# A seven-product first feed-forward block, and all modulation as 1024-column pieces spread over the blocks

## The chip, the core and the metric
The kernel runs on one core of one Trainium2 chip. The metric is the device time of one execution in microseconds. TensorE does the matrix products; VectorE, ScalarE and GpSimd compute beside it; SyncE's queue issues nearly all DMAs, in program order, and waits in place when one of them has to wait. TensorE's granted clock is given as a share of full speed.

## The reference
One inference step of a model of two layers, on 512 latent and 128 context tokens of width 1024. A layer has three residual blocks: a feed-forward block, a mixing block and a second feed-forward block. The mixing block is attention with an mLSTM in layer 0, and a gated short convolution in layer 1. Six blocks follow one another:

```python
def modulation(cond, w, b):
    m = jax.nn.silu(cond) @ w + b
    return m.reshape(cond.shape[0], 1, N_MOD, D_MODEL)
def modulate_in(x, g_pre, mod, j):
    return rmsnorm(x, g_pre) * (1.0 + mod[:, :, 3 * j + 1]) + mod[:, :, 3 * j]
def gated_residual(x, out, g_post, mod, j, weight):
    return x + weight * mod[:, :, 3 * j + 2] * rmsnorm(out, g_post)
def swiglu(h, w13, w2):
    a, g = jnp.split(h @ w13, 2, axis=-1)
    return (jax.nn.silu(g) * a) @ w2
```

The modulation of a layer is nine groups of 1024 columns (shift, scale and gate of each of its three blocks), for two condition vectors, latent and context. Its weight matrix is 1024 by 9216 for each layer. D is 1024 and the hidden width of a feed-forward block is 2816.

## The kernel before, in words
The blocks are numbered s = 0 to 5: feed-forward, mixing ("ab"), feed-forward, feed-forward, short convolution ("sc"), feed-forward. Every matrix product is made with three matmuls: each float32 operand is split into a high part (ScalarE copies it, `w_hi`) and the rest (VectorE subtracts, `w_lo`), and high times high, high times low and low times high are summed.

A feed-forward block has two halves of 11 hidden tiles (`HF`). Each half has an in-phase and an out-phase. In the in-phase a pair of units makes one hidden tile: the two weight tiles of 128 columns for g and a, against 640 tokens in two parts of 320. A unit is 8 times 3 times 2 matmuls of 320 columns, a plain pair 96. A seven-product pair makes the same tile from seven products of half-size blocks (4 times 3 matmuls each, 84 in all). Its operands are sums of blocks: VectorE and GpSimd add weight blocks (`w_sum`), and once for a block VectorE and GpSimd add blocks of the activations (`t_sum`), split into `t_hi` and `t_lo`. The table `PLAIN` says which blocks use it: in those the first half has 3 plain and 8 seven-product pairs, the second half 11 seven-product pairs. Block 0 is not among them: all its 22 pairs are plain.

The out-phase has units of 15 matmuls of 512 columns (five token tiles, three matmuls each). In a second half's out-phase seven of the units for the second 512 columns are held back (`held_hi`, `held_lo`), so that TensorE can finish the output tile after tile, and the next block's normalisation and transposes are placed between these tiles. What this does is the boundary to the next block.

Raw weights have two slots. The load of unit n waits in SyncE's queue for the split of unit n − 2 (`w_lo_ok`), ScalarE's split of unit n waits until TensorE has finished unit n − 2 of an in-phase (n − 4 of an out-phase), and TensorE waits for VectorE's split.

The modulation is made in two ways. In block 0 (`JOBS`) layer 0's last seven groups are made in 28 steps of 256 columns: VectorE multiplies a weight tile with the condition vector's column and accumulates, 16 instructions a step, then transposes and adds (`job_half`, `job_turn`), and TensorE sums over the partitions (`sum_jobs`). For layer 1 (`MODS`) a piece of 1024 columns takes eight steps (`add_step`): each loads a tile of 512 KB (`ada_tile`) and has two VectorE instructions of 1024 columns, one for each condition vector. After a step the semaphore `ada_used` goes up; the load of tile j waits for step j − 3. TensorE then sums the accumulators with 8 matmuls of 256 columns in four column groups (`modulation`), VectorE adds the bias to four rows (`modulation_rows`), SyncE stores them to DRAM (`modulation` there), and the block that needs them loads them as columns (`load_cols`) or as gate rows (`load_gate`). The tables `LOADS`, `STEPS`, `SUMS_AT`, `ROWS_AT`, `STORE_AT` give the unit of an out-phase (in the sc block: of its in-phase) at which each of these stands in its engine's program. The sc block has 24 in-units; units come in threes, and VectorE computes the convolution of a group (`u_pad`, `y_conv`) among the splits.

The first two groups of layer 0 are made in the opening, with `cond_silu` as TensorE's stationary operand, two columns wide.

## Time and profile before

| | |
|---|---|
| three runs, median | 2480.43 us |
| lowest and highest | 2480.0 and 2482.57 us |
| the profiled execution, from its first to its last instruction (its own time; the profile gives no other) | 2483.0 us |
| TensorE busy in it | 2419.5 us |
| VectorE, ScalarE, GpSimd busy | 1773.0, 907.4, 351.1 us |
| mean granted TensorE clock | 0.994 |

Busy time of an engine says little by itself. The windows table cuts the span into stages, and the timeline rows say which engine waited at a place and for whom: a bracket at the end of a row holds the idle time before it and what ended it. A row with xN merges N instructions.

### The profile page before, as it was taken

Reading aid. Unit: us, or ns where it says so; the run is one execution under the profiler, and the core shown is the slowest. Engines: PE = TensorE matmul, PEld = TensorE weight load, DVE = VectorE, ACT = ScalarE, POOL = GpSimd, SP = SyncE. Lnnn points to the kernel's source line nnn. Section 1 sums busy time; section 2 is a strip of 40 time slices with the busy share of each in tenths; the row PEclk is TensorE's granted clock in tenths of the full one; section 3 lists DMA queues with packets and bytes.
Section 4 is the critical chain, followed back from the end, with each engine's and each line's share of the span. In section 5 each row is a group of like instructions: output and inputs, shape, how many; then the busy total and the mean of one; then the engine's idle time right before and its main releaser. Section 6 shows DMA issues by size and latency. Waiting matters only on the chain. (4 is left out here: it accounts for less than half of the span.)

```text
span 2483.0 us, 38913 instructions
## 1 busy us (share of the span) xinstructions
PE 2419.5 (97%) x14856; PEld 2227.7 (90%) x14856; DVE 1773.0 (71%) x2701; ACT 907.4 (37%) x1740; POOL 351.1 (14%) x373
## 2 busy tenths in 40 slices
...
GB/s 246 163 141 136 124 152 165 132 120 145 67 57 73 93 98 94 64 221 98 86 143 96 86 70 211 102 86 107 98 145 137 106 84 100 69 146 101 86 107 114
DMA packets 359638, 289.76 MB, mean 117 GB/s; under 512 B 38918, under 2 KB 317334, under 8 KB 358454
## 3 DMA queue, kind: packets, MB, share of 16 engines
...
HBM read 275.32 MB, written 12.18 MB: 116 GB/s over the span
## 5 line engine op out<-in xcount | busy, mean ns | idle before, releaser
L2064 DVE TENSOR_TENSOR w_lo<-w_raw,w_hi 128x512 fp32r<-128x512 f32 (+2 forms) x287 | 260.8, 912 | 281.0 <-ACT w_hi L1458 278.0
L1458 ACT ACTIVATE w_hi<-w_raw 128x512 fp32r<-128x512 f32 (+2 forms) x287 | 228.6, 799 | 602.5 <-DMA w_raw<-in_ffn_w_dram 231.4
L969 PE MATMUL psum<-w_hi,act_hi 128*128 128x512 f32 x800 | 319.1, 399 | 4.8 <-DVE w_lo L2064 4.8
L971 PE MATMUL psum<-w_hi,act_lo 128*128 128x512 f32 x800 | 317.1, 396 | 0.0
L970 PE MATMUL psum<-w_lo,act_hi 128*128 128x512 f32 x800 | 317.0, 396 | 0.0
L1044 PE MATMUL psum<-hT_hi,w_hi 128*128 128x320 f32 x1216 | 278.0, 310 | 0.6 <-DVE w_lo L2064 0.4
L1044 PE MATMUL psum<-hT_lo,w_hi 128*128 128x320 f32 x1216 | 277.1, 309 | 0.0
L1044 PE MATMUL psum<-hT_hi,w_lo 128*128 128x320 f32 x1216 | 277.0, 309 | 0.0
L1088 PE MATMUL psum<-hT_hi,w_hi 128*128 128x320 f32 x684 | 211.6, 309 | 1.6 <-DVE z_quarters L2348 1.6
L1090 PE MATMUL psum<-hT_hi,w_lo 128*128 128x320 f32 x684 | 211.4, 309 | 0.0
L1089 PE MATMUL psum<-hT_lo,w_hi 128*128 128x320 f32 x684 | 211.3, 309 | 0.0
L1044 PEld LDWEIGHTS psum<-hT_hi,w_hi 128*128 128x128 f32 x1216 | 203.0, 188 | 3.5 <-DVE w_lo L2064 2.6
L1044 PEld LDWEIGHTS psum<-hT_hi,w_lo 128*128 128x128 f32 x1216 | 203.4, 188 | 0.0
L1044 PEld LDWEIGHTS psum<-hT_lo,w_hi 128*128 128x128 f32 x1216 | 203.2, 188 | 0.0
L969 PEld LDWEIGHTS psum<-w_hi,act_hi 128*128 128x128 f32 x800 | 150.6, 188 | 46.5 <-DVE w_lo L2064 8.9
L971 PEld LDWEIGHTS psum<-w_hi,act_lo 128*128 128x128 f32 x800 | 150.6, 188 | 36.7
L970 PEld LDWEIGHTS psum<-w_lo,act_hi 128*128 128x128 f32 x800 | 150.7, 188 | 35.4
L2033 DVE SCALAR_TENSOR_TENSOR mod_acc<-ada_raw,cond_silu,mod_acc 128x256 f32<-128x256 f32 x392 | 159.9, 479 | 0.0
L1088 PE MATMUL psum<-t_hi,w_hi_more 128*128 128x320 f32 x456 | 140.9, 309 | 0.0
L1090 PE MATMUL psum<-t_hi,w_lo_more 128*128 128x320 f32 x456 | 140.9, 309 | 0.0
L1089 PE MATMUL psum<-t_lo,w_hi_more 128*128 128x320 f32 x456 | 140.8, 309 | 0.0
L1088 PEld LDWEIGHTS psum<-hT_hi,w_hi 128*128 128x128 f32 x684 | 128.4, 188 | 2.3 <-DVE w_lo_more L2310 2.3
...
## 6 DMA issues: line engine op xcount, KB each, us to landing
w_raw<-in_ffn_w_dram SPq DMA_DIRECT2D x116, 512.0 KB, 4.4
w_raw<-in_ffn_w_dram SPq DMA_DIRECT2D x148, 256.0 KB, 2.9
w_raw_next<-in_ffn_w_dram SPq DMA_DIRECT2D x60, 512.0 KB, 5.4
ada_raw<-in_ada_w_dram SPq DMA_DIRECT2D x56, 512.0 KB, 3.6
ada_tile_ffn<-in_ada_w_dram SPq DMA_DIRECT2D x40, 512.0 KB, 4.1
w_raw<-in_ab_w_in_dram SPq DMA_DIRECT2D x28, 512.0 KB, 4.1
w_raw<-in_sc_w_in_dram SPq DMA_DIRECT2D x24, 512.0 KB, 4.0
...
```

Of the source, the lines that this page charges most:

```text
L969: mm(out, a_hi, b_hi, start=first, stop=False)
L970: mm(out, a_hi, b_lo, start=False, stop=False)
L971: return mm(out, a_lo, b_hi, start=False, stop=final)
L1044: last = mm(IN[p][0:width, h, 0:HT], a, b[:, k, h * HT:(h + 1) * HT], start=(k == 0 and a is hi and b is hT_hi), stop=(k == KD - 1 and a i ...
L1088: mm(out, hi[:, k, :], o_hi[:, k, :], start=(k == 0 and q < 4), stop=False, **on)
L1089: mm(out, hi[:, k, :], o_lo[:, k, :], start=False, stop=False, **on)
L1090: last = mm(out, lo[:, k, :], o_hi[:, k, :], start=False, stop=(k == KH - 1), **on)
L1458: A(dst, src, ACT.Copy).then_inc(w_hi_ok, 1)
L2033: ins = V.scalar_tensor_tensor(acc[:, cd, :], w, col, acc[:, cd, :], ALU.mult, ALU.add)
L2064: V.tensor_tensor(d_, a, b.bitcast(F32), ALU.subtract).then_inc(w_lo_ok, 1)
```

## The change
- Block 0 becomes a seven-product block like blocks 2, 3 and 5: 3 plain and 8 seven-product pairs, then 11.
- The 256-column steps are gone. The gate of block 0 (group 2 of layer 0) is multiplied on TensorE: eight tiles of 512 KB (`ada_direct`), four in flight, and 32 matmuls of 256 columns with `cond_silu` stationary, 16 behind unit 3 and 16 behind unit 5.
- The other six groups become pieces in the manner of layer 1's, and layer 1's groups move along. Pieces in the first and second half or block: block 0 has 2 and 1, ab 2, block 2 has 2 and 1 (before 2 and 0), block 3 has 2 and 1 (before 2 and 0), sc 3 (before 2), block 5 has 1 and 0. The second half's piece is of kind "rest"; its accumulators and tiles lie in the place of the operand sums and of x.
- In a second half with a piece, three of the five tiles of x are reloaded after the piece's last step, and the next block's columns are loaded after the piece has been stored.
- In the sc block the third piece has its steps at units 18 to 22, its sum in the out-phase after unit 4, its rows at unit 6, its store and the next block's columns ahead of the load of unit 8.

```diff
-PLAIN = {2: (3, 0), 3: (3, 0), 5: (3, 0)}
+PLAIN = {0: (3, 0), 2: (3, 0), 3: (3, 0), 5: (3, 0)}
...
-JOBS = {0: (0, 2 * D, (HF, HF), (3, 3))}
-assert (sum(JOBS[0][2]) + sum(JOBS[0][3])) * JW == NMOD - 2 * D
-MODS = {1: [[(1, 0), (1, D)]], 2: [[(1, 2 * D), (1, 3 * D)], []], 3: [[(1, 4 * D), (1, 5 * D)], []],
-        4: [[(1, 6 * D), (1, 7 * D)]], 5: [[(1, 8 * D)], []]}
-assert sorted(z for q in MODS.values() for y in q for z in y) == [(1, j * D) for j in range(9)]
+GATE0 = (0, 2 * D)
+MODS = {0: [[(0, 3 * D), (0, 4 * D)], [(0, 5 * D)]], 1: [[(0, 6 * D), (0, 7 * D)]], 2: [[(0, 8 * D), (1, 0)], [(1, D)]],
+        3: [[(1, 2 * D), (1, 3 * D)], [(1, 4 * D)]], 4: [[(1, 5 * D), (1, 6 * D), (1, 7 * D)]], 5: [[(1, 8 * D)], []]}
+assert sorted([GATE0] + [z for q in MODS.values() for y in q for z in y]) == [(0, j * D) for j in range(2, 9)] + [(1, j * D) for j in range(9)]
 MW, MODC = 256, 1024
-STEPS = {"ffn": [1 + j for j in range(16)], "ab": [2, 2, 3, 3, 4, 4, 5, 5, 7, 9, 10, 10, 11, 11, 12, 12], "sc": [2 + j for j in range(16)]}
-SUMS_AT = {"ffn": (10, 18), "ab": (6, 12), "sc": (11, 19)}
-ROWS_AT = {"ffn": (13, 21), "ab": (7, 99), "sc": (13, 21)}
-STORE_AT = {"ffn": (15, 99), "ab": (9, 15), "sc": (15, 23)}
-LOADS = {"ffn": [3, 3, 3] + [4 + j for j in range(13)], "ab": [4, 4, 5, 5, 5, 6, 6, 7, 7, 8, 8, 10, 12, 13, 13, 13],
-         "sc": [2, 2, 2] + [4 + j for j in range(13)]}
-LATE = (3, 0)
+STEPS = {"ffn": [1 + j for j in range(16)], "rest": [1 + j for j in range(8)],
+         "ab": [2, 2, 3, 3, 4, 4, 5, 5, 7, 9, 10, 10, 11, 11, 12, 12], "sc": [2 + j for j in range(16)] + [18, 18, 19, 19, 20, 20, 21, 22]}
+SUMS_AT = {"ffn": (10, 18), "rest": (9,), "ab": (6, 12), "sc": (11, 19, 99)}
+ROWS_AT = {"ffn": (13, 21), "rest": (12,), "ab": (7, 99), "sc": (13, 21, 99)}
+STORE_AT = {"ffn": (15, 99), "rest": (13,), "ab": (9, 15), "sc": (15, 23, 99)}
+LOADS = {"ffn": [3, 3, 3] + [4 + j for j in range(13)], "rest": [3, 3, 3] + [4 + j for j in range(5)],
+         "ab": [4, 4, 5, 5, 5, 6, 6, 7, 7, 8, 8, 10, 12, 13, 13, 13], "sc": [2, 2, 2] + [4 + j for j in range(13)] + [17, 17, 18, 18, 19, 19, 20, 21]}
+SC_LAST = (4, 6, 8)
+DIRECT_LOADS = {2: (0, 1), 3: (2, 3), 4: (4, 5), 5: (6, 7)}
+DIRECT_AT = {3: (0, 1, 2, 3), 5: (4, 5, 6, 7)}
...
+            def load_direct(k):
+                if k >= 4:
+                    sp.wait_ge(direct_used, k - 3)
+                else:
+                    sp.wait_ge(xT_ok, NT)
+                layer, col = GATE0
+                src = ada_w[layer].rearrange("(p k) n -> p k n", k=KD)[:, k, col:col + MODC]
+                dma(direct[k % 4][:], src).then_inc(direct_loaded[k % 4], 16)
...
+                        if n < 2:
+                            continue
                         sp.wait_ge(w_lo_ok, n - 1)
                         dma(raw[:, n % 2], src[:, :, col + i * P:col + (i + 1) * P]).then_inc(w_loaded[n % 2], 16)
-                    if i == 0 and done is not None:
-                        store_rows(done)
-                    for t in range(NT) if i == 1 else ():
+                        for k in DIRECT_LOADS.get(n, ()):
+                            load_direct(k)
+                    if s == 0 and i == 1:
+                        load_bias_rows(0, "ffn", *GATE0)
+                    for t in range(NT) if i == 1 and s else ():
...
+                    if s == 0 and g == ph["g0"] + 1 and not ph["half"]:
+                        store_mod_rows(0, "ffn", *GATE0)
+                        load_slow()
...
+                        load_pairs(s, ffn_w13[l, f], ph, c0)
+                        if ph["half"] == 0:
+                            load_out(s, ffn_w2[l, f], c0, ph)
+                            continue
+                        load_out(s, ffn_w2[l, f], c0, ph, 0, 4)
+                        sp.wait_ge(pe_prod, SEVEN * ph["g1"])
+                        sp.wait_ge(mod_stored, STORED(ph["mb"] - 1))
+                        load_gate(s)
+                        if not ph["mods"]:
                             for t in range(NT):
                                 load_out(s, ffn_w2[l, f], c0, ph, 4 + 2 * t, 6 + 2 * t)
-                                dma(X[:, t, :], xd[:, t, :]).then_inc(s_x, 16)
+                                reload_x(s, t)
                             load_out(s, ffn_w2[l, f], c0, ph, 4 + 2 * NT)
                             continue
-                        load_in(ffn_w13[l, f], nb, 0, HF, [FF + c0, c0], P, ph, done)
-                        done = ph if ph["jobs"] else None
-                        if ph["half"] == 1:
-
-                            sp.wait_ge(mod_stored, 16 * ph["bt"])
-                            load_gate(s)
-                            if s + 1 < len(SUBS):
-                                load_cols(s + 1)
-                        elif s == 0:
-                            load_slow()
-                        load_out(s, ffn_w2[l, f], c0, ph)
+                        for t in range(2):
+                            load_out(s, ffn_w2[l, f], c0, ph, 4 + 2 * t, 6 + 2 * t)
+                            reload_x(s, t)
+                        load_out(s, ffn_w2[l, f], c0, ph, 8)
+                        sp.wait_ge(ada_used, USED(AG(ph, 8 * len(ph["mods"]) - 1)))
+                        for t in range(2, NT):
+                            reload_x(s, t)
+                        sp.wait_ge(mod_stored, STORED(ph["mods_end"] - 1))
+                        load_cols(s + 1)
...
+                        sp.wait_ge(mod_stored, STORED(ph["mods_end"] - 2))
+                        sp.wait_ge(ada_used, USED(AG(ph, 8 * len(ph["mods"]) - 1)))
+                        load_gate(s)
+                        load_out(s, sc_w_out[0], 0, ph, 0, SC_LAST[2])
+                        store_mod_rows(ph["mods_end"] - 1, "sc", *ph["mods"][-1])
                         sp.wait_ge(mod_stored, STORED(ph["mods_end"] - 1))
-                        load_gate(s)
                         load_cols(s + 1)
-                        load_out(s, sc_w_out[0], 0, ph)
+                        load_out(s, sc_w_out[0], 0, ph, SC_LAST[2])
...
+            def direct_gate(n):
+
+                for k in DIRECT_AT.get(n, ()):
+                    pe.wait_ge(direct_loaded[k % 4], 16 * (k // 4 + 1))
+                    for i in range(4):
+                        last = mm(PS[32 * i:32 * i + 2, DIRECT_BANK, 0:MW], csil[:, :, k], direct[k % 4][:, i * MW:(i + 1) * MW], start=(k == 0), stop=(k == KD - 1))
+                    last.then_inc(mod_mm if k == KD - 1 else direct_used, 1)
...
+                    elif ph["kind"] == "sc" and u == SC_LAST[0]:
+                        modulation(ph, None, last_of=len(ph["mods"]) - 1)
...
+                                direct_gate(ph["nin"] + 2 * i + r)
...
-            def job_half(ph, q, h, i=0, turn=True):
-
-                j = ph["jb"] + q
-                dve.wait_ge(ada_loaded[h], (i + (j + 1)) * 16)
-                if h == 1:
-                    own.wait_back(0)
-                for k in range(KD // 2):
...
+                    elif ph["kind"] == "sc" and u == SC_LAST[1]:
+                        modulation_rows(ph["mods_end"] - 1, "sc", SUM_BANK["sc"][-1])
...
+                if s == 0 and ph["plain"]:
+                    modulation_rows(0, "ffn", DIRECT_BANK)
```

**SyncE, block 0, units 2 to 5 of the first half.** `w_raw` are the units' weights, `ada_direct` the gate's tiles. After the change:

```order
L584 DMA ada_direct0_146<-in_ada_w_dram 128x1024 [waits xT_ok]
L584 DMA ada_direct1_147<-in_ada_w_dram 128x1024 [waits xT_ok]
L584 DMA w_raw_52<-in_ffn_w13_dram 128x8x128 [waits w_lo_ok]
L584 DMA ada_direct2_148<-in_ada_w_dram 128x1024 [waits xT_ok]
L584 DMA ada_direct3_149<-in_ada_w_dram 128x1024 [waits xT_ok]
L584 DMA mod_bias_ffn_170<-in_ada_b_dram 2x256 x4
L584 DMA w_raw_52<-in_ffn_w13_dram 128x8x128 [waits w_lo_ok]
L584 DMA ada_direct0_146<-in_ada_w_dram 128x1024 [waits direct_used]
L584 DMA ada_direct1_147<-in_ada_w_dram 128x1024 [waits direct_used]
L584 DMA w_raw_52<-in_ffn_w13_dram 128x8x128 [waits w_lo_ok]
L584 DMA ada_direct2_148<-in_ada_w_dram 128x1024 [waits direct_used]
L584 DMA ada_direct3_149<-in_ada_w_dram 128x1024 [waits direct_used]
```

The weights of unit 5 (the third `w_raw`) stand behind two of the gate's tiles that wait for `direct_used`. Before, two 256-column tiles with waits of their own stood between these loads.

**SyncE, block 2, second half's out-phase, from unit 2's weights on.** Before:

```order
L589 DMA w_raw_52<-in_ffn_w2_dram 128x512 [waits w_lo_ok] x2
L589 DMA held_raw0_100<-in_ffn_w2_dram 128x512 [waits pe_unit,act_ready]
L589 DMA gate_56<-modulation 128x2x1024 [waits x_new,mod_stored,pe_prod]
L589 DMA g_post_57<-in_norm_g_dram 128x1024
L589 DMA mod_cols_64<-modulation 128x2x8 x2
L589 DMA g_pre_65<-in_norm_g_dram 128x8
L589 DMA w_raw_52<-in_ffn_w2_dram 128x512 [waits w_lo_ok] x2
L589 DMA x_49<-x_kept_rows 128x1024
L589 DMA w_raw_52<-in_ffn_w2_dram 128x512 [waits w_lo_ok]
```

After, from the wait for the last product on:

```order
L584 DMA mod_bias_rest_172<-in_ada_b_dram 2x256 [waits mrow_ok,pe_prod]
L584 DMA mod_bias_rest_172<-in_ada_b_dram 2x256 x3
L584 DMA ada_tile_rest2_139<-in_ada_w_dram 128x1024
L584 DMA ada_tile_rest0_137<-in_ada_w_dram 128x1024
L584 DMA ada_tile_rest1_138<-in_ada_w_dram 128x1024
L584 DMA held_raw0_93<-in_ffn_w2_dram 128x512 [waits pe_unit,act_ready]
L584 DMA gate_56<-modulation 128x2x1024 [waits x_new,mod_stored,pe_prod]
L584 DMA g_post_57<-in_norm_g_dram 128x1024
L584 DMA w_raw_52<-in_ffn_w2_dram 128x512 [waits w_lo_ok]
L584 DMA ada_tile_rest2_139<-in_ada_w_dram 128x1024 [waits ada_used]
L584 DMA w_raw_52<-in_ffn_w2_dram 128x512 [waits w_lo_ok]
L584 DMA ada_tile_rest0_137<-in_ada_w_dram 128x1024 [waits ada_used]
```

The piece's bias rows and three column tiles (`ada_tile_rest`) came ahead of the held weights and the gate, each further tile came behind a unit's weights, and the block's columns (`mod_cols`, `g_pre`) left this place.

**SyncE, sc block, from unit 16's weights on.** Before (`x7` are units 17 to 23):

```order
L589 DMA w_raw_52<-in_sc_w_in_dram 128x8x128 [waits w_lo_ok]
L589 DMA ada_tile_sc0_148<-in_ada_w_dram 128x1024 [waits ada_used0]
L589 DMA w_raw_52<-in_sc_w_in_dram 128x8x128 [waits w_lo_ok] x7
L589 DMA modulation<-mod_rows_sc_165 2x256 [waits mrow_ok]
L589 DMA modulation<-mod_rows_sc_165 2x256 x3
```

After, from unit 17's weights on:

```order
L584 DMA w_raw_52<-in_sc_w_in_dram 128x8x128 [waits w_lo_ok]
L584 DMA ada_tile_sc2_145<-in_ada_w_dram 128x1024 [waits ada_used]
L584 DMA ada_tile_sc0_143<-in_ada_w_dram 128x1024 [waits ada_used]
L584 DMA w_raw_52<-in_sc_w_in_dram 128x8x128 [waits w_lo_ok]
L584 DMA ada_tile_sc1_144<-in_ada_w_dram 128x1024 [waits ada_used]
L584 DMA ada_tile_sc2_145<-in_ada_w_dram 128x1024 [waits ada_used]
L584 DMA w_raw_52<-in_sc_w_in_dram 128x8x128 [waits w_lo_ok]
L584 DMA ada_tile_sc0_143<-in_ada_w_dram 128x1024 [waits ada_used]
L584 DMA ada_tile_sc1_144<-in_ada_w_dram 128x1024 [waits ada_used]
L584 DMA w_raw_52<-in_sc_w_in_dram 128x8x128 [waits w_lo_ok]
L584 DMA ada_tile_sc2_145<-in_ada_w_dram 128x1024 [waits ada_used]
```

Two tiles with waits for `ada_used` now stand between the weights of units 17, 18, 19 and 20, and one behind each of the next.

**VectorE, sc block, from unit 18's split on.** Before:

```order
L2064 TENSOR_TENSOR w_lo_54<-w_raw_52,w_hi_53 128x1024 [waits w_hi_ok,s_dve]
L2503 TENSOR_TENSOR u_tmp_59<-psum,y_conv_88 128x320 [waits pe_unit]
L2503 TENSOR_TENSOR u_tmp_59<-psum,y_conv_88 128x192
L2503 TENSOR_TENSOR u_tmp_59<-psum,y_conv_88 128x128
L2440 CAST act_hi_85<-u_tmp_59 128x640 [waits in_evac1]
L2441 TENSOR_TENSOR act_lo_86<-u_tmp_59,act_hi_85 128x640 [waits s_dve]
L2064 TENSOR_TENSOR w_lo_54<-w_raw_52,w_hi_53 128x1024 [waits w_hi_ok,act_ready]
L2064 TENSOR_TENSOR w_lo_54<-w_raw_52,w_hi_53 128x1024 [waits w_hi_ok]
```

After:

```order
L1947 TENSOR_TENSOR w_lo_54<-w_raw_52,w_hi_53 128x1024 [waits w_hi_ok,s_dve]
L2111 TENSOR_SCALAR mod_acc_sc20_164<-ada_tile_sc2_145,cond_silu_72 128x1024 [waits ada_landed2]
L2111 TENSOR_SCALAR mod_acc_sc21_165<-ada_tile_sc2_145,cond_silu_72 128x1024
L2113 SCALAR_TENSOR_TENSOR mod_acc_sc20_164<-ada_tile_sc0_143,cond_silu_72,mod_acc_sc20_164 128x1024 [waits ada_used,ada_landed0]
L2113 SCALAR_TENSOR_TENSOR mod_acc_sc21_165<-ada_tile_sc0_143,cond_silu_72,mod_acc_sc21_165 128x1024
L2344 TENSOR_TENSOR u_tmp_59<-psum,y_conv_85 128x320 [waits pe_unit]
L2344 TENSOR_TENSOR u_tmp_59<-psum,y_conv_85 128x192
L2344 TENSOR_TENSOR u_tmp_59<-psum,y_conv_85 128x128
L2309 CAST act_hi_82<-u_tmp_59 128x640 [waits in_evac1]
L2310 TENSOR_TENSOR act_lo_83<-u_tmp_59,act_hi_82 128x640 [waits s_dve]
L1947 TENSOR_TENSOR w_lo_54<-w_raw_52,w_hi_53 128x1024 [waits w_hi_ok,act_ready]
L2113 SCALAR_TENSOR_TENSOR mod_acc_sc20_164<-ada_tile_sc1_144,cond_silu_72,mod_acc_sc20_164 128x1024 [waits ada_used,ada_landed1]
```

Two steps of the third piece (`mod_acc_sc20`, `mod_acc_sc21`) came behind unit 18's split and two behind unit 19's; before, the splits of units 19 and 20 stood with nothing between them.

## Rows read from the trace of the kernel before

**Rows 1.** The page, busy time of each engine over the span.
```profile
PE 2419.5 (97%) x14856; PEld 2227.7 (90%) x14856; DVE 1773.0 (71%) x2701; ACT 907.4 (37%) x1740; POOL 351.1 (14%) x373
```

**Rows 2.** Waits of TensorE: waiter, releaser, us in total, times, longest.
```profile
PE psum L969 <- DVE w_lo L2064: 4.8, 8, 1.5
```

**Rows 3.** Windows by stage: window, length, busy time of each engine, clock, DMA.
```profile
56.92:198.43 141.51, 141.06 (x962) 140.80 (x961) 122.46 (x239) 26.82 (x30) 0.00 (x0) 1.00 0.50 143
198.43:276.13 77.70, 77.70 (x337) 62.54 (x336) 43.48 (x87) 14.23 (x22) 0.00 (x0) 1.00 0.42 133
276.13:431.00 154.87, 154.87 (x1057) 154.87 (x1056) 129.45 (x253) 29.54 (x33) 0.00 (x0) 1.00 0.51 153
431.00:534.23 103.23, 100.07 (x496) 82.39 (x495) 75.87 (x123) 42.97 (x97) 18.97 (x33) 1.00 0.34 99
955.29:1054.61 99.32, 98.80 (x674) 98.56 (x673) 85.62 (x120) 47.77 (x86) 23.03 (x14) 1.00 0.25 71
1054.61:1134.68 80.07, 79.90 (x365) 62.54 (x363) 61.04 (x73) 19.14 (x32) 0.00 (x0) 1.00 0.61 196
1134.68:1270.19 135.51, 135.51 (x925) 135.51 (x924) 114.94 (x162) 63.82 (x116) 33.06 (x20) 1.00 0.27 76
1270.19:1370.76 100.57, 98.55 (x492) 82.44 (x491) 51.93 (x65) 43.20 (x96) 18.95 (x31) 1.00 0.42 140
1715.36:1815.60 100.24, 98.55 (x492) 82.42 (x491) 52.10 (x66) 43.10 (x96) 18.71 (x31) 1.00 0.37 119
```

**Rows 4.** Timeline of TensorE, block 2, a piece's sum: start, us, instruction.
```profile
1093.78 1.04 PE L1109 MATMUL psum<-mod_acc_ffn,pick 128*2 128x256 f32 x16
```

**Rows 5.** Timeline of SyncE and VectorE, block 2, first half's out-phase.
```profile
1056.10 1.29 SPq L589 DMA_DIRECT2D ada_tile_ffn<-in_ada_w_dram  x3
1059.89 1.42 DVE L2229 TENSOR_SCALAR mod_acc_ffn<-ada_tile_ffn,cond_silu 128x1024 f32<-128x1024 f32 x2 [1.20 <-DMA ada_tile_ffn<-in_ada_w_dram]
1067.21 0.68 DVE L2064 TENSOR_TENSOR w_lo<-w_raw,w_hi 128x512 fp32r<-128x512 f32 x1
1067.81 2.47 DVE L2231 SCALAR_TENSOR_TENSOR mod_acc_ffn<-ada_tile_ffn,cond_silu,mod_acc_ffn 128x1024 f32<-128x1024 f32 x2
...
1124.17 0.86 DVE L2216 TENSOR_TENSOR mod_rows_ffn<-psum,mod_bias 2x256 f32<-2x256 f32 x2 [3.10 <-PE psum L1109]
```

**Rows 6.** Timeline of VectorE, sc block.
```profile
1929.20 1.22 DVE L2064 TENSOR_TENSOR w_lo<-w_raw,w_hi 128x1024 fp32r<-128x1024 f32 x1
...
1944.86 0.95 DVE L2490 TENSOR_TENSOR u_pad<-psum,silu_g 128x320 f32<-128x320 f32 x3 [4.13 <-PE psum L1044]
...
1948.35 1.23 DVE L2064 TENSOR_TENSOR w_lo<-w_raw,w_hi 128x1024 fp32r<-128x1024 f32 x1
...
1953.08 0.95 DVE L2503 TENSOR_TENSOR u_tmp<-psum,y_conv 128x320 f32<-128x320 f32 x3 [1.82 <-PE psum L1044]
...
1955.45 1.23 DVE L2064 TENSOR_TENSOR w_lo<-w_raw,w_hi 128x1024 fp32r<-128x1024 f32 x1
```

**Rows 7.** Timeline of SyncE and ScalarE, sc block, units 19 and 20.
```profile
1930.46 4.21 SPq L589 DMA_DIRECT2D w_raw<-in_sc_w_in_dram  x2
1930.55 1.06 ACT L1458 ACTIVATE w_hi<-w_raw 128x1024 fp32r<-128x1024 f32 x1 [6.04 <-PE psum L1044]
```

**Rows 8.** The page, DMA issues: count, KB each, median us from issue to landing.
```profile
w_raw<-in_sc_w_in_dram SPq DMA_DIRECT2D x24, 512.0 KB, 4.0
```

**Rows 9.** Timeline, block 2, second half's out-phase: gate's load, TensorE's wait, gate's product.
```profile
1274.73 0.38 SPq L589 DMA_DIRECT2D gate<-modulation  x1
1285.16 0.50 PE L969 MATMUL psum<-w_hi,act_hi 128*128 128x512 f32 x1 [0.77 <-DVE w_lo L2064]
1285.03 2.28 DVE L2082 SCALAR_TENSOR_TENSOR gate<-gate,g_post 128x2048 f32<-128x2048 f32 x1
```

**Rows 10.** Timeline of VectorE, block 2: the same product without and beside GpSimd.
```profile
1271.81 0.83 DVE L2364 TENSOR_TENSOR z_quarters<-z_quarters 128x640 f32<-128x640 f32 x1 [0.59 <-ACT z_quarters L1615]
971.58 1.92 DVE L2364 TENSOR_TENSOR z_quarters<-z_quarters 128x640 f32<-128x640 f32 x1
```

More of the change, by code:

```diff
@@ L37 @@
 PRO = 2 * D // MODW
-JW = 256
 SQ = 32
-JB = JW // SQ
-JOBS_MAX = 14
 EPS = 1e-6
@@ L775, in load_out @@
                         load_mods(ph, u)
-                    z, r = divmod(u - LATE[ph["half"]] if late else u, 3)
-                    if r < 2 and 0 <= z < late:
-                        load_job(ph, jobs + z, parts=(r,))
                     for i in held_at(ph, u):
```

339 lines of the change are left out of this document (82 added, 257 removed).

## The prediction
> **What bounds the kernel now.** I read the busy shares first: TensorE is busy 97% of the span [rows 1]. The waits of TensorE come next: all its waits for split weights in the out-phases make 4.8 us together, in 8 places [rows 2]. So the time is the sum of TensorE's work, plus whatever new waits the change makes. The windows table by stage then gives the price of each stage; its start and end are starts of the first TensorE row of one stage and of the next [rows 3].
>
> The reader is to see three pairs of stages there. Eleven plain pairs (22 units) took 154.87 us, so 14.08 us a pair and 7.04 us a unit; eleven seven-product pairs took 135.51 us, 12.32 a pair. Eight seven-product pairs behind three plain ones took 99.32 us. The first half's out-phase took 77.70 us with the old modulation (22 units, 3.53 us each) and 80.07 us with two 1024-column pieces. The second half's out-phase up to the next block's third unit took 103.23 us in block 0, but 100.57 and 100.24 in blocks 2 and 3.
>
> The sum is made against the profiled span, 2483.0 us. It is 2.6 us above the median of the runs, 2480.43; I subtract the difference from the median.
>
> **The change, block 0, first half.** Before: 10 plain pairs after the first, 141.51 us, and 77.70 us of out-phase, 219.21 together [rows 3]. After:
> - two plain pairs, 28.16 us, and eight seven-product pairs, 99.3;
> - the gate's columns on TensorE: 32 matmuls of 256 columns against a two-column stationary operand. The nearest row is the sum of a 1024-column piece, 8 matmuls of the same form, 1.04 us or 0.98 to the next row's start [rows 4]; four times 0.98 are 3.9 us. They go into four column groups like those, so I take that value; the bounds are 3 and 6;
> - the weights of unit 5. SyncE's queue holds them behind two of the gate's tiles, which wait for the matmuls that follow unit 3. First units end at 56.92, so unit 3 ends at 71.0, and unit 4, behind 2.0 us of gate matmuls, at 80.0. The load of unit 5 goes out at 72.5 behind two 512 KB tiles; a 512 KB load of this form takes 4.0 us alone [rows 8], and three tiles issued together at 1056.10 had the first landed at 1059.89 [rows 5], so I put it at 78.7. ScalarE's split (1.06, [rows 7]) and VectorE's (1.2, [rows 6]) end at 81.0: a wait of 1.0 us (0 to 2.5);
> - VectorE adds the gate's rows (two such additions took 0.86 [rows 5], so four 1.8 us) before the fourth product's weights. Against block 2 it is then up to 1.4 us late, while a seven-product pair leaves it 12.3 minus 10.7 us (85.62 busy in eight pairs) to catch up: 0.5 us. Slow 4-byte loads stand in the queue before the third pair's weights, needed only some 8 us later: 0.3 us (0 to 2.5);
> - the out-phase as in block 2, 80.07.
>
> That is 213.2, a gain of 6.0 us.
>
> **Block 0, second half.** 154.87 becomes 135.51: 19.4 us gained. The out-phase gets one new piece (next part).
>
> **One more piece in the second half's out-phase, blocks 0, 2 and 3.** TensorE: one sum, 1.0 us [rows 4]. VectorE: eight steps in units 1 to 8. A step is 2.4 us (the first 1.4) and a split 0.6 [rows 5], so 3.0 a unit against TensorE's 3.53. The first half already runs so, but here VectorE also has the gate's 2.28 us at unit 4 and the held weights. From the phase's start at 0: the tiles go out at 1.4, behind the bias rows; the first lands 3.8 later as in the first half [rows 5], step 0 ends at 6.6, unit 2's split at 7.2 (needed at 7.05), unit 3's at 10.1, unit 4's weights come as before, behind the 1.5 MB of the gate (TensorE waited 0.77 there, [rows 9]). Then gate 2.28, step 2.4, split 0.6: unit 5's weights are ready 5.3 us after unit 4's, where TensorE needs them after 3.5. Waits: 0.2 + 0.5 + 1.4 + 0.1 = 2.2 us at units 2, 4, 5 and 6, against 0.77 in block 2 and, by its window's 0.33 less [rows 3], 0.44 in block 3. So 1.4 and 1.8 more. Bounds: 0 and 5 each. From unit 6 on VectorE gains half a microsecond a unit.
> The next block's columns are now loaded at the end, behind the rows' store and three tiles of x. TensorE ends the piece's sum at 2.2 + 35.3 + 1.0 = 38.5 and the first output tile at 38.5 + 3.5 + 7.7 = 49.7. From 38.5 on come the rows 1.8, their store and its landing, which I take at 3.5, the columns' issue and landing behind 1.5 MB of x, which I take at 6.7, since gate and columns in this queue made unit 4 wait till 15 from a start at 4.5 [rows 9]: 50.5. VectorE begins the boundary 1 us late; I count half. 0.5 us (0 to 3).
> So block 2 pays 1.0 + 1.4 + 0.5 = 2.9 us and block 3 pays 3.3. Block 0 goes from 103.23 to 100.57 + 2.9 = 103.5, since its own 2.7 us of the old 256-column steps' disturbance go: 0.2 lost.
>
> **The third piece in the short-convolution block.** Its eight steps sit at units 18 to 22, two a unit at first. What is queued behind what decides here. On SyncE the second tile of unit 18 waits for a step that VectorE does after unit 18's split, and unit 19's weights stand behind it; in unit 19 likewise for unit 20's.
> - Unit 17 ends at 1930.5 ([rows 7], what that split waited for) and unit 18's split at 1930.35 [rows 6]. Two steps (1.4 + 2.4) and the convolution's tail (2.37, from 1953.08 to 1955.45) bring VectorE to 1936.4. Unit 19's load goes out at 1932.2 instead of well before 1930.46 [rows 7], lands at 1936.2 to 1937.6, and its two splits end at 1939.1; unit 18 ends at 1937.5. Wait 1.6.
> - Unit 20's load waits for a step behind that split: +2.4 step, +0.5 for the tile's issue, +4.7 landing, +2.2 splits = 9.8, against 7.04 + 1.0 (a sum): wait 1.8.
> - Unit 21 is VectorE's own: product 0.9, two steps 4.8, convolution 2.5 (0.9 and 2.5 together are 1944.86 to 1948.35, [rows 6]), split 1.15 = 9.3 against 7.04: 2.3.
> - Unit 22: rows 1.8, step 2.4, tail 2.3, split 1.15 = 7.6: 0.6.
> Sum 6.3 us (2 if the loads came free, since only the last two waits are VectorE's, unit 21's then 1.2; 10 if each landing takes 1.5 more). In the out-phase: the piece's sum 1.0, and a late weight load, since the queue waits for the rows' store before the columns' load: 1.2 (0 to 3). Block 4 pays 8.5 us.
>
> **Sum.** −6.0 − 19.4 + 0.2 + 2.9 + 3.3 + 8.5 = −10.5 us: 2470 us. The mixing block is left as it is; it has two pieces before and after, at the same units.
>
> **A rule against the change.** VectorE's product of two SBUF tiles took 0.83 us with GpSimd idle and 1.92 us at 971.58, inside eight pairs in which GpSimd was busy 23.03 us [rows 3, 10]. Of the nineteen seven-product pairs of block 0 seventeen will have GpSimd's two weight sums.
> The Trainium skill, "SBUF — State Buffer", section "Who interferes with whom", says that a VectorE instruction with two SBUF inputs and a GpSimd instruction that reads SBUF take an exclusive lock and that the later one blocks fully; the trace agrees with a block of about 1.1 us. If that fell on the path it would be 17 × 1.1 = 19 us and take back the second half's gain.
> Counted from the rows alone: 1.92 − 0.83 = 1.09 us in each of 17 pairs is 18.5 us, and the time would be 2489. But stages with GpSimd's sums ran at 12.32 us a pair with TensorE busy all 135.51 us, so there it is hidden; VectorE's 114.94 us leave room. Chance 0.03.
>
> **The rivals.**
> 1. The sum above, 2464 to 2477. Chance 0.50.
> 2. The new waits are mostly covered. With the lower bounds (block 4 pays 1.9 + 1.0, blocks 2 and 3 pay 1.0 each, block 0's second out-phase gains 1.7, its first half gains 7.8): 7.8 + 19.4 + 1.7 − 2 − 2.9 = 24 us, 2456. For it speaks that TensorE's waits are so small now; against it that unit 21's wait needs only durations of rows. 2456 to 2464: 0.17.
> 3. The waits cost more: block 4 pays 12 (10 + 1 + 1), each second out-phase 2 us more, half a microsecond more at places in block 0: −10.5 + 3.5 + 6 + 1 = 0 net: 2480. For it speaks that loads behind one another in one queue stretched by more than I count; 2477 to 2485: 0.22. No measurable change is mostly this.
> 4. It is slower. Mechanism: in the three second out-phases the first column tiles land late behind the gate's loads and the held weights, VectorE starts its eight steps late, and each microsecond comes back as TensorE's wait at units 2 to 5, since split and step stand in one order. It decides from (2485.4 − 2470) / 3 = 5.1 us a block. A delay of 6 us gives 2488. Against it: the first tile goes out ahead of the gate's load, and in the first half it landed 3.8 us after its issue. 0.08.
>
> **Numbers.** About 0.2%, 5 us, is what measurement can tell. Faster means under 2475.5: rival 2, nearly all of the first case and the least part of the third: 0.69. Same, 2475.5 to 2485.4: 0.20. Slower: 0.11, with the lock. Range: from 2459 to 2480, which leaves out half of case 2, a third of case 3 and case 4, near 0.2.
>
> **What would show it.** In the changed profile: the eight and eleven seven-product pairs of block 0 at 99 to 101 and 135.5 us; the gate's matmuls about 3.9 us; TensorE waiting for split weights about 1 us ahead of unit 5 in block 0, about 1.4 us ahead of unit 5 of the second out-phases, and four waits of 0.5 to 2.5 us in units 19 to 22 of block 4; scaled columns about 1 us after VectorE could have begun a boundary. I would be wrong if seven-product pairs ran above 12.4 us in block 0, if column tiles landed more than 5 us after issue, or if VectorE's double steps were absorbed.

## The result and the profile after

The changed kernel took 2490.61 us (median of six runs, 2489.51 to 2495.45) against 2483.03 for the kernel before (median of six, the three of the forecast among them). The ratio of the means is 1.0037, interval 1.0026 to 1.0049. It is slower. The forecast was 2470 with a range from 2459 to 2480. The profiled executions took 2488.1 and 2483.0 us, 5.1 apart, and the stages below are told in these.

The page's busy times of the changed kernel:

```profile
PE 2406.5 (97%) x14780; PEld 2201.8 (88%) x14780; DVE 1819.7 (73%) x2517; ACT 977.1 (39%) x1901; POOL 413.1 (17%) x409
```

TensorE is busy for 13 us less than before [rows 1], and yet the end comes later: the waits are the subject. The windows table of the changed kernel, with the columns of [rows 3]: block 0 (first half's in-phase behind the first pair, its eight seven-product pairs alone, out-phase; second half's in-phase, out-phase with boundary), the second out-phases of blocks 2 and 3 with boundary, block 4's in-phase and out-phase:

```profile
57.20:191.19 133.99, 131.66 (x930) 128.20 (x929) 115.04 (x147) 57.64 (x97) 28.34 (x16) 1.00 0.34 92
91.31:191.19 99.88, 99.02 (x676) 98.66 (x673) 86.15 (x122) 46.92 (x85) 23.01 (x14) 1.00 0.28 71
191.19:271.11 79.92, 79.89 (x364) 62.54 (x363) 60.95 (x73) 19.02 (x32) 0.00 (x0) 1.00 0.62 196
271.11:406.63 135.52, 135.52 (x926) 135.51 (x924) 114.91 (x162) 63.80 (x116) 33.05 (x20) 1.00 0.27 76
406.63:515.66 109.03, 102.14 (x508) 83.71 (x507) 70.96 (x85) 43.27 (x98) 18.96 (x33) 0.98 0.46 146
1250.44:1358.38 107.94, 102.13 (x509) 83.69 (x508) 72.31 (x85) 43.16 (x96) 18.94 (x31) 0.98 0.50 170
1702.71:1811.61 108.90, 101.90 (x509) 83.62 (x508) 72.64 (x86) 43.16 (x96) 18.72 (x31) 0.98 0.45 149
1811.61:1978.87 167.26, 161.65 (x1091) 158.11 (x1090) 125.47 (x161) 27.04 (x29) 0.00 (x0) 0.98 0.50 151
1978.87:2061.14 82.27, 78.86 (x418) 65.69 (x417) 45.80 (x61) 38.58 (x89) 13.44 (x26) 1.00 0.31 100
```

Block 4 took 158.40 and 82.58 us in the kernel before:

```profile
1815.60:1974.00 158.40, 158.29 (x1091) 155.53 (x1090) 107.46 (x145) 27.06 (x29) 0.00 (x0) 1.00 0.44 133
1974.00:2056.58 82.58, 79.23 (x403) 66.97 (x401) 43.92 (x57) 38.80 (x89) 13.70 (x26) 0.98 0.31 99
```

Against the forecast, term by term (us, minus is gained; before from [rows 3] and the fence above):

| term | forecast | measured |
|---|---|---|
| block 0, first half | −6.0 | 213.91 − 219.21 = −5.3 |
| block 0, second in-phase | −19.4 | 135.52 − 154.87 = −19.4 |
| block 0, second out-phase, boundary | +0.2 | 109.03 − 103.23 = +5.8 |
| block 2, the same | +2.9 | 107.94 − 100.57 = +7.4 |
| block 3, the same | +3.3 | 108.90 − 100.24 = +8.7 |
| block 4 | +8.5 | +8.9 − 0.3 = +8.6 |
| sum | −10.5 | +5.8 |

Three terms of one kind are 15.5 us too small; that is nearly the whole miss. The stages that the table leaves out changed by −0.7 us together.

**Where a boundary loses.** TensorE's waits of the changed kernel; the first row is its waits for the normalised tiles that it transposes:

```profile
PE psum L927 <- DVE part L1990: 16.8, 12, 4.3
PE psum L909 <- DVE w_lo L1947: 9.0, 10, 1.4
PE psum L982 <- DVE w_lo L1947: 7.0, 4, 3.1
```

The timeline of block 2's boundary, SyncE first, then VectorE, then TensorE:

```profile
1285.29 3.53 SPq L584 DMA_DIRECT2D w_raw<-in_ffn_w_dram  x2
1293.17 1.15 SPq L584 DMA_DIRECT2D modulation<-mod_rows_rest  x4
1294.36 0.36 SPq L584 DMA_DIRECT2D w_raw<-in_ffn_w_dram  x1
...
1289.57 0.69 DVE L1947 TENSOR_TENSOR w_lo<-w_raw,w_hi 128x512 fp32r<-128x512 f32 x1
...
1291.38 1.77 DVE L2098 TENSOR_TENSOR mod_rows_rest<-psum,mod_bias_rest 2x256 f32<-2x256 f32 x4
...
1298.23 0.69 DVE L1947 TENSOR_TENSOR w_lo<-w_raw,w_hi 128x512 fp32r<-128x512 f32 x1 [3.76 <-ACT w_hi L1396]
1298.95 3.08 DVE L2020 TENSOR_TENSOR part<-psum,part 128x512 f32<-128x512 f32 x5
1302.52 1.24 DVE L1959 SCALAR_TENSOR_TENSOR mod_cols<-mod_cols,g_pre 128x16 f32<-128x16 f32 x1 [0.49 <-DMA g_pre<-in_norm_g_dram]
...
1314.24 1.80 PE L927 MATMUL psum<-ident,part 128*128 128x128 f32 x8 [3.07 <-DVE part L1990]
1315.69 0.77 PE L909 MATMUL psum<-held_hi,act_hi 128*128 128x512 f32 x1
```

Read it from below. TensorE waits 3.07 us for the first normalised tile. VectorE begins the boundary with five additions at 1298.95, directly behind the split of the last unit's weights, for which it was idle 3.76 us. These weights were issued at 1294.36, behind the store of the piece's rows, and the store waited in SyncE's queue until VectorE had added the rows (1291.38 to 1293.15). The two loads ahead of the store went out by 1288.8, and the last unit's slot was free from 1290.26, when VectorE had split the weights two units before (1289.57 + 0.69): the store held the load for 4.1 us. For the columns, which the forecast took for the late ones, VectorE waited 0.49 us, less than the 1 us that I said.

The first transposes start 15.29 us after the additions (1298.95 to 1314.24). In blocks 0 and 3 it is 15.29 too (456.08 to 471.37, 1752.43 to 1767.72), and in block 0 of the kernel before (475.46 to 490.75): the additions, ScalarE's squares, GpSimd's five gate products, the norm, x, the next norm. This chain took the same time in all four. In the kernel before it ended 0.2 us behind TensorE in block 0. In block 2 it would have ended at 1311.64 + 15.29 = 1326.93, 0.5 us ahead of TensorE, so there was next to nothing left to hide a later start. Of the kernel before, VectorE's additions and TensorE's first transposes in block 0, the same in block 2 with the second transposes, and last the second transposes of block 2 in the changed kernel:

```profile
475.46 3.08 DVE L2137 TENSOR_TENSOR part<-psum,part 128x512 f32<-128x512 f32 x5
490.75 1.16 PE L989 MATMUL psum<-ident,part 128*128 128x128 f32 x8 [0.20 <-DVE part L2107]
...
1311.64 3.08 DVE L2137 TENSOR_TENSOR part<-psum,part 128x512 f32<-128x512 f32 x5
1327.39 1.05 PE L989 MATMUL psum<-ident,part 128*128 128x128 f32 x8
1334.94 1.13 PE L989 MATMUL psum<-ident,part 128*128 128x128 f32 x8 [0.89 <-issue]
...
1322.54 1.13 PE L927 MATMUL psum<-ident,part 128*128 128x128 f32 x8
```

The gap of 0.89 us ahead of the second transposes is gone where TensorE has waited ahead of the first; why is not shown.

The wait isn't all of the price. The first row is the stretch behind it, the second the one behind the longest wait of block 4; the clock is the third number from the end:

```profile
1314.24:1332.00 17.76, 17.76 (x80) 14.64 (x81) 11.02 (x13) 9.22 (x24) 4.41 (x8) 0.90 0.00 0
1936.85:1946.70 9.85, 9.85 (x51) 9.66 (x54) 5.41 (x5) 1.06 (x1) 0.00 (x0) 0.71 0.69 207
```

A mean of 0.90 of 2.4 GHz, with the lower level at 1.2 GHz, is a loss of 0.10 × 17.76 = 1.8 us; behind the wait of 3.10 us in block 4 it is 0.29 × 9.85 = 2.9. The 0.77 us matmul above took 0.40 elsewhere. Block 2's 7.4 us are then: sum 1.0, waits at units 2, 4 and 5 of 0.15 + 0.81 + 1.42 against 0.77 before, 1.6; the boundary's wait 3.1; the clock 1.8; less the gap of 0.9. That is 6.6; the other 0.8 us I can't assign.

### The profile page after: what moved, and what is told of

Read it like the earlier page. It is cut to its first block and busy times, and to the rows that moved or that the text cites. A ratio compares the mean times of both kernels' runs of the same rounds, so it can differ in the third digit from the quotient of the medians.

```text
span 2488.1 us, 38245 instructions
## 1 busy us (share of the span) xinstructions
PE 2406.5 (97%) x14780; PEld 2201.8 (88%) x14780; DVE 1819.7 (73%) x2517; ACT 977.1 (39%) x1901; POOL 413.1 (17%) x409
## 5 line engine op out<-in xcount | busy, mean ns | idle before, releaser
L1396 ACT ACTIVATE w_hi<-w_raw 128x512 fp32r<-128x512 f32 (+1 forms) x249 | 188.1, 760 | 528.7 <-DMA w_raw<-in_ffn_w_dram 247.6
L1947 DVE TENSOR_TENSOR w_lo<-w_raw,w_hi 128x512 fp32r<-128x512 f32 (+1 forms) x249 | 214.3, 862 | 218.8 <-ACT w_hi L1396 217.4
L1028 PE MATMUL psum<-hT_hi,w_hi 128*128 128x320 f32 x912 | 282.2, 309 | 2.4 <-DVE z_quarters L2215 2.4
L1030 PE MATMUL psum<-hT_hi,w_lo 128*128 128x320 f32 x912 | 281.8, 309 | 0.0
L1029 PE MATMUL psum<-hT_lo,w_hi 128*128 128x320 f32 x912 | 281.8, 309 | 0.0
L1028 PE MATMUL psum<-t_hi,w_hi_more 128*128 128x320 f32 x608 | 187.9, 309 | 0.0
L1030 PE MATMUL psum<-t_hi,w_lo_more 128*128 128x320 f32 x608 | 187.9, 309 | 0.0
L1856 POOL TENSOR_TENSOR w_sum<-w_raw 128x512 f32<-128x512 f32 x36 | 54.9, 1524 | 776.8 <-DVE w_lo L2177 776.8
L1028 PEld LDWEIGHTS psum<-hT_hi,w_hi 128*128 128x128 f32 x912 | 171.2, 188 | 3.5 <-DVE w_lo_more L2177 3.3
L982 PE MATMUL psum<-hT_hi,w_hi 128*128 128x320 f32 x608 | 141.3, 314 | 7.1 <-DVE w_lo L1947 7.0
L982 PE MATMUL psum<-hT_lo,w_hi 128*128 128x320 f32 x608 | 139.5, 311 | 0.0
L982 PE MATMUL psum<-hT_hi,w_lo 128*128 128x320 f32 x608 | 139.3, 311 | 0.0
L2231 DVE TENSOR_TENSOR z_quarters<-z_quarters 128x640 f32<-128x640 f32 x76 | 128.4, 1690 | 4.8 <-ACT z_quarters L1554 4.8
```

What stands on the lines that cost most here:

```text
L982: last = mm(IN[p][0:width, h, 0:HT], a, b[:, k, h * HT:(h + 1) * HT], start=(k == 0 and a is hi and b is hT_hi), stop=(k == KD - 1 and a i ...
L1028: mm(out, hi[:, k, :], o_hi[:, k, :], start=(k == 0 and q < 4), stop=False, **on)
L1029: mm(out, hi[:, k, :], o_lo[:, k, :], start=False, stop=False, **on)
L1030: last = mm(out, lo[:, k, :], o_hi[:, k, :], start=False, stop=(k == KH - 1), **on)
L1396: A(dst, src, ACT.Copy).then_inc(w_hi_ok, 1)
L1856: pool.tensor_tensor(S1[:], A21(g), A22(g), ALU.add).then_inc(ws_ok, 1)
```

## The experiments

Each is an edit of the changed kernel, compared with the kernel before in the same runs. "Gained" is against 2490.6. The kernel before had medians of 2483.51 us beside experiments 1 to 4, 2482.02 beside 5 to 8 and 2483.86 beside 9 and 10, so differences between these groups are good to about 1 us.

**1. The store behind the last weights.**

```diff
-STORE_AT = {... "rest": (13,), ...}
+STORE_AT = {... "rest": (14,), ...}
```

> The store of the piece's rows in the second halves of blocks 0, 2 and 3 stands behind the last unit's weights in SyncE's queue, not ahead of them. Theory (queue): the last unit's weights wait for VectorE's rows, their split comes some 4 us late, VectorE begins the boundary behind it, and nothing on the way to the first transposes has slack. Then the three waits of TensorE ahead of the transposes (4.28, 3.07, 3.88 us) fall under 0.5 each and the lowered clock behind them goes too: 12 to 15 us less than the changed kernel, 2476 to 2479, below the kernel before. Rival (late columns): the columns' loads come behind the same store either way, so the three waits stay as they are and the time stays at 2490.

2478.47 us, ratio 0.9981 (0.9972 to 0.9990): 12.1 gained by one number, and faster than the kernel before. Windows of the three second out-phases, and block 2's SyncE and VectorE:

```profile
406.60:511.06 104.46, 100.60 (x508) 82.36 (x507) 70.79 (x85) 43.31 (x98) 18.95 (x33) 1.00 0.46 152
1247.14:1350.76 103.62, 100.30 (x509) 82.40 (x507) 71.09 (x85) 43.13 (x96) 18.95 (x31) 1.00 0.52 177
1694.80:1799.89 105.09, 100.40 (x508) 82.36 (x507) 71.26 (x86) 43.09 (x96) 18.74 (x31) 1.00 0.47 154
```

```profile
1282.60 4.83 SPq L584 DMA_DIRECT2D w_raw<-in_ffn_w_dram  x3
1289.99 1.15 SPq L584 DMA_DIRECT2D modulation<-mod_rows_rest  x4
...
1291.92 3.08 DVE L2020 TENSOR_TENSOR part<-psum,part 128x512 f32<-128x512 f32 x5
1298.26 0.17 DVE L1959 SCALAR_TENSOR_TENSOR mod_cols<-mod_cols,g_pre 128x16 f32<-128x16 f32 x1 [3.27 <-DMA g_pre<-in_norm_g_dram]
```

The three loads now go out together, the clock is 1.00, and the blocks lost 4.6, 4.3 and 3.8 us less. The gap of 0.89 us ahead of the second transposes is back in all three, which is one reason why it is less than wait and clock together. The additions start right behind the last split. The columns are waited for longer than before the edit, 3.27 us against 0.49, and it costs nothing: TensorE waits no more than 0.20 us for the first transposes, since VectorE has nothing else to do while GpSimd's products run. So a late column isn't what the boundary hangs on; the late last weights are.

**2. Columns and x early, store where it was.**

```diff
+early = 11 if s == 0 else 99
-load_out(s, ffn_w2[l, f], c0, ph, 8)
+load_out(s, ffn_w2[l, f], c0, ph, 8, early)
 ... reload_x(s, t) for t in range(2, NT)
+if s == 0:
+    load_cols(1)
+    load_out(s, ffn_w2[l, f], c0, ph, early)
```

> In block 0 alone x's last three tiles and the next block's columns are loaded ahead of unit 11's weights, some 15 us earlier; the rows' store stays ahead of the last unit's weights. Rival (late columns or late x hold VectorE at the boundary): the wait of 4.28 us ahead of the transposes in block 0 goes, blocks 2 and 3 keep theirs, the time is 5 us lower, 2485. Theory (queue): scaled columns come earlier but the wait stays within 0.5 us of 4.28, and the time stays at 2490.

2493.41 us, ratio 1.0042 (1.0028 to 1.0055). VectorE and TensorE at block 0's boundary:

```profile
460.30 3.08 DVE L2025 TENSOR_TENSOR part<-psum,part 128x512 f32<-128x512 f32 x5
463.30 0.16 DVE L1964 SCALAR_TENSOR_TENSOR mod_cols<-mod_cols,g_pre 128x16 f32<-128x16 f32 x1
...
475.60 1.87 PE L932 MATMUL psum<-ident,part 128*128 128x128 f32 x8 [4.48 <-DVE part L1995]
```

The columns are there at once and the wait is 4.48 us, as it was. The rival is out. The early loads stood ahead of unit 11's weights, and TensorE waited 2.0 and 0.9 us there that it had not waited before; these 2.9 us are about what the time lies above 2490.6.

**3. Block 4, the third piece's loads later, its steps where they were.**

```diff
-"sc": [...] + [17, 17, 18, 18, 19, 19, 20, 21]
+"sc": [...] + [17, 18, 19, 20, 20, 21, 21, 22]
```

> Short-convolution block: the third piece's steps stay in their units on VectorE, only its tile loads stand later in SyncE's queue, so that none waits for a step ahead of the next unit's weights. Theory (queue): the wait of 3.10 us ahead of unit 19 goes with the lowered clock behind it (0.71 over 9.85 us), some 5 to 6 us, and the waits of 1.9 and 0.5 us at units 21 and 22, which are VectorE's own, stay: 2485. Rival (VectorE's double steps hold all of these units): the wait at unit 19 stays above 2 us and the time at 2490.

2484.55 us, ratio 1.0004 (0.9995 to 1.0013): 6.1 gained. The in-phase:

```profile
1811.00:1972.28 161.28, 159.11 (x1091) 155.54 (x1089) 125.47 (x161) 27.05 (x29) 0.00 (x0) 1.00 0.52 157
```

Unit 19's wait of 3.10 us is gone with its clock; 1.44 and 0.53 us stay at units 21 and 22. Queue and VectorE each have their own share, and they are apart now: 6.0 and 2.9 us of the 8.9.

**4. Block 4, steps spread.**

```diff
-"sc": [2 + j for j in range(16)] + [18, 18, 19, 19, 20, 20, 21, 22]
+"sc": [2, 3, 4, 4, 5, 6, 7, 7, 8, 9, 10, 10, 11, 12, 13, 13, 14, 15, 16, 16, 17, 18, 19, 20]
```

The load of tile j stands two units behind step j − 3.

> Short-convolution block: all three pieces' steps are spread over units 2 to 20, with two in one unit only where VectorE is idle afterwards (units 4, 7, 10, 13, 16), each tile's load placed so that it never blocks the next weights. Theory: the third piece then costs its sum of 1.0 us and little else, all waits in units 19 to 22 go, 8 us less than the changed kernel, 2482. Rival (24 steps don't fit beside 23 splits and the convolution, whatever their order): the waits move to units 4 to 16 and at least half of the 8.9 us stays, 2486 or more.

2480.50 us, ratio 0.9993 (0.9984 to 1.0002): 10.1 gained. The in-phase:

```profile
1811.12:1968.93 157.81, 157.76 (x1091) 155.53 (x1089) 125.36 (x161) 27.06 (x29) 0.00 (x0) 1.00 0.53 160
```

TensorE is busy in all of it, and VectorE does the same 125.4 us of work. 24 steps fit; their places, and those of their loads, were the cost.

**5. Both edits.** Experiments 1 and 4 together.

> The store behind the last unit's weights and the spread steps of the short-convolution block together. Theory: the two losses are in different blocks and add: 2490.6 minus 12.1 minus 10.1 is 2468.4, ratio 0.994 to the kernel before, TensorE waits over 2 us nowhere behind the mixing block. Rival (one gives back what the other gains, since every block inherits the arrival times of the last): 2473 or more.

2469.31 us, ratio 0.9945 (0.9931 to 0.9958). The sum of the two gains would give 2468.4: they add.

**6. No step beside the gate's product.** On top of experiment 5.

```diff
-STEPS: "rest": [1 + j for j in range(8)]      SUMS_AT: "rest": (9,)
+STEPS: "rest": [1, 2, 3, 5, 6, 7, 8, 9]       SUMS_AT: "rest": (10,)
```

> As e5_store_and_spread, and in the second halves of blocks 0, 2 and 3 no step of the piece in unit 4, in which VectorE also multiplies the gate tile (steps in units 1 to 3 and 5 to 9, the sum a unit later). Theory (VectorE's order): the wait of 1.43 us ahead of unit 5 goes in all three, 4 us less than e5_store_and_spread: 2464.5. Rival (the weights land late, whatever VectorE does, since the DMA engines are 0.9 busy there): the waits at units 4 and 5 stay above 1.5 us together, no gain.

2467.30 us, ratio 0.9936 (0.9922 to 0.9949), 2.0 below experiment 5, within the spread of runs. The wait of 1.43 us at unit 5 went in all three blocks, as the theory had it, and came back at the boundary. VectorE and TensorE, block 0:

```profile
448.83 1.31 DVE L2098 TENSOR_TENSOR mod_rows_rest<-psum,mod_bias_rest 2x256 f32<-2x256 f32 x3 [0.73 <-PE psum L1059]
...
452.57 3.08 DVE L2020 TENSOR_TENSOR part<-psum,part 128x512 f32<-128x512 f32 x5
...
467.85 1.16 PE L927 MATMUL psum<-ident,part 128*128 128x128 f32 x8 [1.36 <-DVE part L1990]
```

From 452.57 to 467.85 it is 15.28 us again. My expectation had not followed the fixed chain. Counted from unit 4's start, VectorE's additions moved by −0.6, +0.4 and −0.1 us against experiment 5, where TensorE saved 1.4. The edit also puts the piece's sum a unit later, and VectorE waits 0.73 us for it ahead of the rows.

**7. The gate's tiles 4 and 5 behind unit 5's weights.** On top of experiment 5.

```diff
-DIRECT_LOADS = {2: (0, 1), 3: (2, 3), 4: (4, 5), 5: (6, 7)}
+DIRECT_LOADS = {2: (0, 1), 3: (2, 3), 5: (4, 5, 6, 7)}
```

> As e5_store_and_spread, and in block 0 the gate's tiles 4 and 5 are loaded behind unit 5's weights, not ahead. Theory: the wait of 0.9 to 1.9 us ahead of unit 5 of block 0 goes and nothing takes its place, 1.5 us less than e5_store_and_spread: 2467. Rival: the gate's matmuls behind unit 5 or the first product's weights then wait for the late tiles, no gain or up to 2 us more.

2467.33 us, ratio 0.9937 (0.9923 to 0.9950), 2.0 below experiment 5, again within the spread of runs. In the trace the wait of 1.90 us that experiment 5 has there is gone: no wait is left ahead of unit 5 of block 0, and none appears at the gate's matmuls.

**8. All four.**

> All four edits of tables together: 2490.6 minus 12.1, 10.1, 4 and 1.5 is 2463, if they add; 2468 if the last two give nothing. Lower than the kernel before by 0.6 to 0.8%.

2464.34 us, ratio 0.9929 (0.9915 to 0.9942). The second out-phases with boundary, and block 4's in-phase:

```profile
404.16:507.51 103.35, 100.14 (x508) 82.50 (x507) 71.07 (x85) 43.31 (x98) 18.95 (x33) 1.00 0.47 154
1242.27:1345.82 103.55, 100.25 (x509) 82.51 (x507) 71.15 (x85) 43.17 (x96) 18.92 (x31) 1.00 0.52 177
1689.67:1793.56 103.89, 100.26 (x508) 82.51 (x507) 71.33 (x86) 43.09 (x96) 18.68 (x31) 1.00 0.47 156
1793.56:1951.36 157.80, 157.75 (x1091) 155.52 (x1089) 125.34 (x161) 27.05 (x29) 0.00 (x0) 1.00 0.54 160
```

**9 and 10. The rows later.** On top of experiment 8. In experiment 9 `ROWS_AT` of the second halves is 13; in 10 the rows stand behind the five additions, with the two further moves that its expectation names.

> As e8_all_four, and VectorE adds the bias to the piece's rows a unit later, in unit 13 of the three second out-phases (in e8_all_four it waited 0.7 us for the sum in unit 12, and the first transposes came 1.4 us late in each boundary). Theory (what VectorE does ahead of its first addition of the boundary is paid by TensorE one for one, once the slack is gone): the waits of 1.4 us ahead of the transposes halve or go, 2 to 4 us less than e8_all_four, 2461. Rival (the boundary's chain starts with the last weights' landing, whatever VectorE does before): no change, 2464.

> As e8_all_four, but the rows stand behind the five additions that begin the boundary, the scaling of the columns behind the first tile's gate product, and x's last tiles ahead of the rows' store. Theory: the additions start 1.8 to 2.5 us earlier and the waits of 1.4 us ahead of the first transposes go, three times: 2460 to 2461. Rival (the columns then land too late for ScalarE's scaled copy of the first transposed tile): new waits of 1 to 4 us ahead of the second transposes or the next block's first unit, 2464 or more.

Experiment 9: 2464.68 us, ratio 0.9924 (0.9910 to 0.9937). The boundary waits went in blocks 0 and 2 and halved in block 3, but unit 4 of block 0's second out-phase waited 2.33 us for weights, against 0.55 in experiment 8; no gain is shown. Experiment 10: 2461.70 us, ratio 0.9910 (0.9895 to 0.9926), the lowest median; its interval overlaps those of experiments 8 and 9. VectorE, block 0:

```profile
450.46 3.07 DVE L2021 TENSOR_TENSOR part<-psum,part 128x512 f32<-128x512 f32 x5
453.46 1.76 DVE L2101 TENSOR_TENSOR mod_rows_rest<-psum,mod_bias_rest 2x256 f32<-2x256 f32 x4
...
460.15 0.37 DVE L1960 SCALAR_TENSOR_TENSOR mod_cols<-mod_cols,g_pre 128x16 f32<-128x16 f32 x1 [2.72 <-DMA g_pre<-in_norm_g_dram]
```

The first transposes waited 0.30 us in block 0 and not in the two others, and the later columns were hidden once more. Unit 4's wait was there too (1.54, 0.56 and 0.60 us); in block 0 it lies between 0.4 and 2.3 in the runs and depends on the landing of its weights, which this study did not pull apart.

## Why the prediction was wrong

- **Block 0's products: right.** Second in-phase 135.52 us against 135.51, out-phase 79.92 against 80.07, the gate's matmuls 3.7 us (71.64 to 73.48 and 89.47 to 91.31) against 3.9, unit 5's wait 1.46 against 1.0. The first half's term is 0.7 off.
- **The step that failed** is "VectorE begins the boundary 1 us late; I count half. 0.5 us (0 to 3)", in three blocks. It followed the rows' store to the columns that stand behind it and left out the weights of the last unit, which stand between them in the same queue, though VectorE's first addition comes behind their split. In its place: the additions start 3.8 us later than with the store behind the weights (456.08 against 452.27 in block 0), TensorE waits 3.1 to 4.3 us, and the lower clock adds 1.7 to 1.8. Moving the store gave back 4.6, 4.3 and 3.8 us, where the forecast had counted 0.5 for the late start. Experiment 1 shows the place, experiment 2 that it isn't the columns. The bound of 3 us had neither the whole delay nor the clock.
- **Rival 4 had the stage and the size right and the mechanism wrong.** It needed 5.1 us a block and gave 2488; the three blocks lost 5.6, 4.5 and 5.4 us above the forecast. But it put the loss at units 2 to 5 by late column tiles. Those waits were 2.4 us in block 2 against 2.2 forecast. I gave it 0.08.
- **The waits at units 2 to 5** were right in size and kind (VectorE's order at unit 5, 1.42 against 1.4). Experiment 6 shows that removing one alone returns most of it at the boundary, which the sum could not have shown.
- **Block 4: right in the sum by luck.** 8.6 against 8.5 us. The waits in the in-phase were 3.1, 0, 1.9 and 0.5 us, where the forecast had 1.6, 1.8, 2.3 and 0.6: unit 19's weights came later than I said, unit 20's were not late. The clock added 2.9 that I did not have. The out-phase should have cost 2.2 and came out 0.3 shorter, and this is the clock too. In both kernels TensorE waits 1.6 us for a tile at the entry to block 5; the stretch behind it, first in the kernel before, then in the changed one:

```profile
2035.77:2045.67 9.90, 9.10 (x52) 8.94 (x53) 7.38 (x8) 5.25 (x13) 2.50 (x4) 0.83 0.38 117
2041.87:2051.77 9.90, 9.10 (x65) 8.94 (x65) 7.37 (x8) 5.25 (x13) 2.50 (x4) 1.00 0.36 117
```

  The kernel before lost 0.17 × 9.90 = 1.7 us there and the changed one nothing, so the out-phase paid 1.4 of the 2.2. Nothing in the change is shown to raise this clock: experiments 5 to 9 had 0.83 at this place again, experiments 1 to 4 and 10 had 1.00. The bound "2 if the loads came free, since only the last two waits are VectorE's" held: 1.4 and 0.5 us in experiment 3.
- **The shared port.** VectorE's product of two SBUF tiles took this in block 0's second half, with GpSimd summing weights beside it:

```profile
285.57 1.92 DVE L2231 TENSOR_TENSOR z_quarters<-z_quarters 128x640 f32<-128x640 f32 x1
```

  That is 1.09 us more than alone [rows 10]; 15 of block 0's nineteen such products took 1.92 us, not the 17 that I counted. The stage has TensorE busy for 135.52 of 135.52 us, so it is hidden. The lock's 2489 is close to the measured time, and only by chance: no stage in which it would act was slow. By the Trainium skill, "SBUF — State Buffer", section "Who interferes with whom", the block itself was to be expected; the trace agrees with the block, and shows that it cost nothing.
- **The base.** The forecast went by the median 2480.43 of three runs; six gave 2483.03. With that base the sum would have said 2472.5. It is 2.6 us of the 20.6; 15.5 us are the boundaries. The other 2.5 us are that the medians lie 7.6 us apart where the two profiled spans lie 5.1 apart: the spread of the runs.
- **The signs.** The sign "if column tiles landed more than 5 us after issue" came true and was not the cause. The median was 5.2 us for the new pieces' tiles, but VectorE waited for a tile only at the first step of each piece, 1.1 to 1.6 us, and that step ended at 6.6 us in block 0 (413.24 − 406.63), as forecast. The row of the page:

```profile
ada_tile_rest<-in_ada_w_dram SPq DMA_DIRECT2D x24, 512.0 KB, 5.2
```

- **The range** left out more than the "near 0.2" that I wrote: half of case 2, a third of case 3, case 4 and the lock are 0.09 + 0.07 + 0.08 + 0.03 = 0.27 by my own chances, and 2480 leaves out five eighths of 2477 to 2485, not a third.
